# Retention of two heads at once: where the rests of queries, keys and values are taken, and the cast of the rotated keys ahead of the values in even heads

## The chip, the cores and the metric

The kernel runs on one core of one Trainium2 chip. The metric is the device time of one execution in microseconds. All times here are in microseconds (us) unless marked otherwise.

## The reference, cut to what matters

The program is a stack of one mixed block (a recurrent part, dilated attention, cross attention, a feed-forward part) and of two layers of a second block. The change touches only the retention of the second block's two layers:

```python
def retention_branch(q, k, v, g):
    qh = rotary(q.reshape(B, S, RET_HEADS, RET_DK)) * (RET_DK ** -0.5)
    kh = rotary(k.reshape(B, S, RET_HEADS, RET_DK))
    ...
    fwd = chunk_retention(qh, kh, vh, decay_logs(DECAY_OFFSET_FWD), strict=False)
    bwd = flip(chunk_retention(flip(qh), flip(kh), flip(vh), decay_logs(DECAY_OFFSET_BWD), strict=True))
    y = fwd + bwd
    y = (y - mean(y)) * rsqrt(var(y) + EPS)      # per token and head
    return y * silu(g)
```

There are four heads of width 256, 512 tokens, and a model width of 1024. Over the whole sequence, both directions together are a 512 x 512 matrix of scores (keys times queries), each multiplied by a decay that depends only on the distance of the two tokens, and then multiplied with the values. This is how the kernel computes it.

## The kernel before, in words

**Three products for one.** Every matrix product is made in full precision out of three fast ones. Each operand x is split into a high part (x cast to the rounded type) and a rest (x minus the high part); the products are high by high, high by rest and rest by high. ScalarE (ACT) makes the high parts by casts, VectorE (DVE) makes the rests of activations by subtractions, and GpSimd (POOL) makes the rests of the weights (`w_lo`, line 720, four pieces of 256 columns for a unit).

**Weights.** All weights come in units of 128 x 1024 numbers, in the order in which TensorE (PE) uses them. A unit is loaded by SyncE (SP) into one of three slots of `w_raw`, cast by ACT into one of five slots of `w_hi` (`cast_to`, line 1650) and gets its rest from POOL (`w_lo`). PE waits for the rest of a unit before the first matmul that uses it (`low_made`). Which unit ACT casts when is written into ACT's program: `follow(t)` for a tile t casts up to three units past the last unit of t, and `take_values` casts the last unit of the value tiles itself before it takes the first of them. A tile of queries, keys or gates has one unit (eight blocks of 128 x 128, 24 matmuls); the four tiles of values (one for each 128 tokens, 512 columns, that is the values of two heads at once) share four units, two blocks of each unit in each tile, so the fourth unit is first used by the seventh of the eight blocks of the first value tile.

**Order of the work.** Every engine follows its own written-out list with semaphore waits; nothing is scheduled at run time, and a waiting instruction holds all that stand behind it on its engine. PE's list for the retention of a layer is: query, key and value tiles of head 0; then for each head `hd`: its two gate tiles, a wait for the rests (`ret_low`, line 1559), the scores (lines 1566 to 1568, 24 matmuls), the two query tiles of the next head, the products with the values (lines 1580 to 1582), the first key tile of the next head, the sums of squares (line 1591), the second key tile, the spread of the inverse deviation (line 902), and, if the next head is even, its four value tiles. Values are computed in even heads for two heads: `RV` for this head and `RV_NEXT` for the one that follows.

**Between PE's tiles.** DVE rotates the queries and the keys out of PSUM (`rotate`, lines 3110 to 3115, six operations); ACT casts them to their high parts (`rotated_high`, line 2192), takes the values (`take_values`, lines 2177 and 2179 for each tile, then the cast of line 2182) or, ahead of odd heads, only casts the second half that is already there (`take_next_values`, line 2187); DVE subtracts (`rest`, line 3120) in the order query, values, key. DVE also multiplies the scores with the decay (line 3138), scales the outputs of the head with the gates (line 3154) and with the inverse deviation (line 3158), and makes their rests (line 2318). PE may start the scores of head n when 5n + 3 rests are counted: those of query, values and keys.

Of the kernel before, what the change touches and what calls it, by code (L numbers as in the profile page):

```python
# [32 lines left out]
XH = 4  # L33
# [202 lines left out]
def build_program(nc, plan, ap, out):  # L236
# [19 lines left out]
    with ctx:  # L256
# [5 lines left out]
        def sem(name):  # L262
            if name not in sems:
                sems[name] = ctx.enter_context(nc.semaphore(name))
            return sems[name]
# [151 lines left out]
        RQ = take(2, S)  # L417
        RKY = take(2, S)
        RV = take(TC, 256)
# [327 lines left out]
        def _(pe):  # L747
# [727 lines left out]
            for l in range(LAYERS):  # L1475
# [80 lines left out]
                for hd in range(XH):  # L1556
                    n = XH * l + hd
                    head_tiles(hd, "g")
                    pe.wait_ge(sem("ret_low"), 5 * n + 3)
                    for c in range(TC):  # L1560

                        if TC * n + c >= 2:
                            pe.wait_ge(sem("ret_masked"), TC * n + c - 1)
                        for k in range(2):
                            o, cols = banks[4 + c % 2][:], slice(c * P, (c + 1) * P)
                            nc.tensor.matmul(o, RK_HI[:, k, cols], RQ_HI[:, k, :], start=(k == 0), stop=False)  # L1566
                            nc.tensor.matmul(o, RK_HI[:, k, cols], RQ_LO[:, k, :], start=False, stop=False)  # L1567
                            mm = nc.tensor.matmul(o, RK_LO[:, k, cols], RQ_HI[:, k, :], start=False, stop=(k == 1))  # L1568
                        mm.then_inc(sem("ret_raw"), 1)
                    if hd + 1 < XH:  # L1570
                        head_tiles(hd + 1, "q")
                    else:
                        gate_tile(f"ret_out{l}", f"n1_{l}", 0)
                    pe.wait_ge(sem("ret_low"), 5 * n + 5)
                    if hd:
                        pe.wait_ge(sem("tmp_ready"), splits[f"ret{l}"][0] + 2 * hd)
                    for d in range(2):
                        for c in range(TC):
                            o, cols, high = banks[6 + d][:], slice(P * d, P * (d + 1)), RP_HI[:, c // 2, c % 2, :]
                            nc.tensor.matmul(o, RV_HI[:, c, cols], high, start=(c == 0), stop=False)  # L1580
                            nc.tensor.matmul(o, RV_HI[:, c, cols], RP_LO[:, c, :], start=False, stop=False)  # L1581
                            mm = nc.tensor.matmul(o, RV_LO[:, c, cols], high, start=False, stop=(c == TC - 1))
                        mm.then_inc(sem("ret_y"), 1)

                    if hd + 1 < XH:
                        tile(stages[f"ret_k{l}_{hd + 1}"][0], splits[f"n1_{l}"][0])
                    else:
                        gate_tile(f"ret_out{l}", f"n1_{l}", 1, range(0, KT // 2))
                    pe.wait_ge(sem("ret_sq_sum"), n + 1)
                    for c in range(TC):  # L1590
                        mm = nc.tensor.matmul(banks[5][:, c:c + 1], ROT[:, 2, c * P:(c + 1) * P], ones[:, 0:1], start=True,
                                              stop=True)
                    mm.then_inc(sem("ret_var"), 1)

                    if hd + 1 < XH:
                        tile(stages[f"ret_k{l}_{hd + 1}"][0] + 1, splits[f"n1_{l}"][0])
                    else:
                        gate_tile(f"ret_out{l}", f"n1_{l}", 1, range(KT // 2, KT))
                    pe.wait_ge(sem("ret_copied"), 2 * n + 2)
                    spread(banks[6])  # L1600
                    if hd + 1 < XH and hd % 2:
                        head_tiles(hd + 1, "v")
# [21 lines left out]
        def _(act):  # L1624
# [496 lines left out]
            for l in range(LAYERS):  # L2121
# [67 lines left out]
                def rotated_high(hd, i, dst, src):  # L2189

                    act.wait_ge(sem("rotated"), 2 * (XH * l + hd) + i + 1)
                    done(nc.scalar.copy(dst, src), "ret_high")

                for hd in range(XH):
                    n = XH * l + hd
                    for what in "qk":
                        for t in range(*stages[f"ret_{what}{l}_{hd}"]):
                            follow(t)
                    if hd == 0:
                        act.wait_ge(sem("gate_used"), counts["gate_ready"])  # L2200
                        act.dma_start(COS, ap["rotary"][:, 0, :]).then_inc(sem("ret_tables"), 16)
                        act.dma_start(SIN, ap["rotary"][:, 1, :]).then_inc(sem("ret_tables"), 16)
                    else:
                        act.wait_ge(sem("ret_masked"), TC * n)
                    act.dma_start(STRIP, ap["strips"][hd]).then_inc(sem("strip_landed"), 16)
                    if hd == 0:
                        rotated_high(0, 0, RQ_HI, RQ)
                        take_values(0)
                        rotated_high(0, 1, RK_HI, RKY)
                    for t in range(*stages[f"ret_g{l}_{hd}"]):  # L2210
                        i = t - stages[f"ret_g{l}_{hd}"][0]
                        if n:
                            act.wait_ge(sem("tmp_ready"), splits[f"ret{l}"][0] + 2 * hd)
                        take_tile(t, RG[:, i, :], func=ACT.Silu)
                    ahead_tiles = list(range(*stages[f"ret_q{l}_{hd + 1}"]) if hd + 1 < XH else
                                       plan.gates[f"ret_out{l}"][0][0:2])
                    follow(ahead_tiles[0])
                    for i in range(2):
                        act.wait_ge(sem("ret_masked"), TC * n + 2 * i + 2)
                        done(nc.scalar.copy(RP_HI[:, i], RP[:, 2 * i:2 * i + 2, :]), "ret_high")  # L2220
                    follow(ahead_tiles[1])
                    for d in range(2):
                        act.wait_ge(sem("ret_y"), 2 * n + d + 1)
                        done(nc.scalar.activation(ROT[:, 2 + d, :], banks[6 + d][:], ACT.Square), "ret_sq")
                    for d in range(2):
                        done(nc.scalar.copy(RY[:, d, :], banks[6 + d][:]), "ret_copied")
                    if hd + 1 < XH:
                        for t in range(*stages[f"ret_k{l}_{hd + 1}"]):
                            follow(t)
                        rotated_high(hd + 1, 0, RQ_HI, RQ)  # L2230
                        if hd % 2:
                            take_values(hd + 1)
                        else:
                            take_next_values(hd + 1)
                        rotated_high(hd + 1, 1, RK_HI, RKY)
                    for d in range(2):
                        high(splits[f"ret{l}"][0] + 2 * hd + d)
                gates(plan.gates[f"ret_out{l}"][0])
# [44 lines left out]
        def _(dve):  # L2283
# [67 lines left out]
            def spread_out():  # L2351

                dve.wait_ge(sem("spread"), counts["stats_ready"])
# [697 lines left out]
            for l in range(LAYERS):  # L3051
# [65 lines left out]
                def rest(count, dst, x, hi):  # L3117

                    dve.wait_ge(sem("ret_high"), count)
                    do(V_.tensor_tensor(dst, x, hi.bitcast(F32), ALU.subtract), "ret_low")  # L3120

                def rests(hd):

                    n = 5 * (XH * l + hd)
                    rest(n + 1, RQ_LO, RQ, RQ_HI)
                    rest(n + 2, RV_LO, RV_NEXT if hd % 2 else RV, RV_HI)
                    rest(n + 3, RK_LO, RKY, RK_HI)

                dve.wait_ge(sem("ret_tables"), 32 * (l + 1))
                rotate(0, "q", RQ)  # L3130
                rotate(0, "k", RKY)
                rests(0)
                for hd in range(XH):
                    n = XH * l + hd
                    dve.wait_ge(sem("strip_landed"), 16 * (n + 1))
# [10 lines left out]
                    dve.wait_ge(sem("ret_var"), n + 1)  # L3146
                    statistic(banks[5][:, 0:TC], 256, TC, EPS)
                    if hd + 1 < XH:
                        rotate(hd + 1, "k", RKY)
                    for t in range(*stages[f"ret_g{l}_{hd}"]):  # L3150
                        evacuated(dve, t)
                    dve.wait_ge(sem("ret_copied"), 2 * n + 2)
                    for d in range(2):
                        do(V_.tensor_tensor(RY[:, d, :], RY[:, d, :], RG[:, d, :], ALU.mult))
                    spread_out()
                    for d in range(2):
                        q = splits[f"ret{l}"][0] + 2 * hd + d
                        do(V_.tensor_tensor(tmp[:, q % 2, :], RY[:, d, :], banks[6][:], ALU.mult), "tmp_ready")
                    for d in range(2):
                        low(splits[f"ret{l}"][0] + 2 * hd + d)  # L3160
                    if hd + 1 < XH:
                        rests(hd + 1)
                for j0, j1 in ((0, KT - 2), (KT - 2, KT - 1), (KT - 1, KT)):
                    gated_pairs(f"ret_out{l}", False, j0, j1)
                    for j in range(j0, j1):
# [174 lines left out]
```

## Time and profile before

| | |
|---|---|
| median of three runs | 3012.26 us (3008.8 to 3012.26) |
| the profiled execution | 3010.7 us, its span 3008.9 us |
| PE busy | 2978.3 us, 99% of the span |
| DVE, ACT, POOL busy | 51%, 37%, 53% |
| granted TensorE clock, mean | 0.999 |
| PE waiting for the rests of line 3120 ahead of the scores | 9.9 us in 6 waits |

An engine's busy time is the time in which at least one of its instructions runs. PE counts matmuls, and PEld the loads of their stationary operands, which run beside the matmuls. Matmul ends are modelled: a matmul shows 0.39 us where the next begins 0.23 us after it.

### The profile page before, as it was taken

How to read it: one execution, taken by the hardware profiler on the slowest of the kernel's cores; microseconds unless marked ns; L12 is line 12 of the kernel's file. 1: busy time of each engine (PE TensorE's matmuls, PEld its weight loads, DVE VectorE, ACT ScalarE, POOL GpSimd, SP SyncE). 2: the span in 40 equal slices, each digit the busy share in tenths (PEclk: the TensorE clock that was granted, in tenths of full speed). 3: DMA queues.
4: the chain of work that ended last, by engine and by line, in shares of the span. 5: the costliest groups of instructions: out<-in, count | busy, mean ns of one | idle time of the engine just before them, and what ended most of it. 6: DMA issues, size and time to landing. Idle time of an engine off the chain costs nothing.

```text
span 3008.9 us, 49790 instructions
## 1 busy us (share of the span) xinstructions
PE 2978.3 (99%) x19898; PEld 2488.9 (83%) x19898; DVE 1537.9 (51%) x2179; ACT 1102.7 (37%) x1665; POOL 1589.7 (53%) x1911
## 2 busy tenths in 40 slices
PE   9999999999999999999999999999999999999998
PEld 7877777788898888988787898888988887888887
DVE  5477887435457777731334274435612443383635
ACT  4454444334442233432433243323433333342323
POOL 6423223357458777554444566556455445565654
PEclk9999999999999999999999999999999999999999
DMA  5211111333327777223222323232223222233322
GB/s 174 84 44 42 48 48 59 98 134 126 98 93 265 261 249 258 84 85 111 83 80 73 92 89 107 91 99 94 81 93 106 78 78 84 92 98 98 98 94 75
DMA packets 91749, 319.49 MB, mean 106 GB/s; under 512 B 10096, under 2 KB 14320, under 8 KB 91264
## 3 DMA queue, kind: packets, MB, share of 16 engines
q1 hardware_dynamic: 84256, 301.34, 30.7%
q10 hardware_dynamic: 7264, 14.98, 1.5%
q8 instruction: 158, 2.59, 0.4%
q14 instruction: 71, 0.58, 0.1%
HBM read 312.32 MB, written 3.93 MB: 105 GB/s over the span
## 4 chain that ended last, share of the span: by engine, by line
PE 90%; DVE 4%; POOL 3%; issue 2%; ACT 1%; DMA 0%; ACTq 0%; POOLq 0%; DVEq 0%; SPq 0%
PE bank L789 24%; PE bank L793 24%; PE bank L790 24%; POOL w_lo L720 2%; PE bank L1056 2%; PE bank L782 2%; PE bank L784 2%; PE bank L783 2%; PE bank L1067 1%; PE bank L1075 1%; DVE arena_r L3120 1%; PE bank L1566 1%; PE bank L1567 1%; PE bank L1568 1%; PE bank L1581 0%
## 5 line engine op out<-in xcount | busy, mean ns | idle before, releaser
L720 POOL TENSOR_TENSOR w_lo<-w_raw,w_hi 128x256 fp32r<-128x256 f32 x1864 | 1541.2, 861 | 1097.8 <-ACT w_hi L1650 1085.3
L789 PE MATMUL bank<-act,w_hi 128*128 128x512 f32 (+1 forms) x3776 | 1423.6, 377 | 7.2 <-POOL w_lo L720 3.9
L793 PE MATMUL bank<-act,w_lo 128*128 128x512 f32 (+1 forms) x3776 | 1401.6, 371 | 0.0
L790 PE MATMUL bank<-act,w_hi 128*128 128x512 f32 (+1 forms) x3776 | 1400.5, 371 | 0.0
L789 PEld LDWEIGHTS bank<-act,w_hi 128*128 128x128 f32 x3776 | 711.4, 188 | 140.0 <-issue 11.6
L793 PEld LDWEIGHTS bank<-act,w_lo 128*128 128x128 f32 x3776 | 711.2, 188 | 122.6
L790 PEld LDWEIGHTS bank<-act,w_hi 128*128 128x128 f32 x3776 | 712.0, 189 | 114.2
L1650 ACT CAST w_hi<-w_raw 128x1024 fp32r<-128x1024 f32 x468 | 487.3, 1047 | 458.2 <-DMA w_raw<-in_weights 202.3
L1658 ACT ACTIVATE arena<-bank 128x512 f32<-128x512 f32 (+1 forms) x177 | 104.3, 593 | 413.7 <-PE bank L793 397.1
L738 POOL TENSOR_TENSOR stats<-stats,exponent 128x8 f32<-128x8 f32 (+2 forms) x39 | 47.0, 1205 | 316.1 <-DVE stats L2349 151.3
L2318 DVE TENSOR_TENSOR act<-tmp,act 128x512 fp32r<-128x512 f32 (+1 forms) x164 | 137.1, 836 | 92.8 <-ACT act L1677 87.2
L3017 DVE SCALAR_TENSOR_TENSOR arena<-arena,small 128x1024 f32<-128x1024 f32 x93 | 140.3, 1509 | 3.3
L3179 DVE TENSOR_SCALAR arena<-arena,params 128x512 f32<-128x512 f32 x88 | 53.0, 602 | 170.2 <-ACT arena L1658 169.8
L1677 ACT CAST act<-tmp 128x512 fp32r<-128x512 f32 (+1 forms) x164 | 95.5, 585 | 121.3 <-DVE tmp L2924 32.0
L2912 DVE TENSOR_TENSOR arena<-arena,bank 128x512 f32<-128x512 f32 x32 | 22.0, 688 | 230.5 <-PE bank L793 230.5
L2485 DVE SCALAR_TENSOR_TENSOR arena<-bank,small,arena 128x512 f32<-128x512 f32 x48 | 36.1, 751 | 166.8 <-PE bank L793 166.6
L1913 ACT ACTIVATE arena<-bank 128x512 f32<-128x512 f32 (+1 forms) x104 | 64.8, 631 | 114.5 <-PE bank L1075 97.1
L3182 DVE SCALAR_TENSOR_TENSOR arena<-arena,params 128x512 f32<-128x512 f32 x88 | 83.0, 943 | 3.1
L782 PE MATMUL bank<-w_hi,act 128*128 128x512 f32 (+1 forms) x224 | 84.6, 378 | 0.0
L784 PE MATMUL bank<-w_hi,act 128*128 128x512 f32 (+1 forms) x224 | 83.7, 374 | 0.0
L783 PE MATMUL bank<-w_lo,act 128*128 128x512 f32 (+1 forms) x224 | 83.7, 374 | 0.0
L3181 DVE SCALAR_TENSOR_TENSOR arena<-arena,params 128x512 f32<-128x512 f32 x88 | 70.6, 802 | 3.1
(299 smaller groups left out, 2557.3 us busy)
## 6 DMA issues: line engine op xcount, KB each, us to landing
w_raw<-in_weights SPq DMA_DIRECT2D x469, 512.0 KB, 3.7
arena<-in_ada SPq DMA_DIRECT2D x96, 512.0 KB, 4.7
arena<-in_strips ACTq DMA_DIRECT2D x8, 448.0 KB, 4.2
arena<-in_x ACTq DMA_DIRECT2D x1, 2048.0 KB, 11.0
y_scratch<-tmp ACTq DMA_DIRECT2D x7, 256.0 KB, 2.0
arena<-y_scratch ACTq DMA_DIRECT2D x1, 1792.0 KB, 8.2
arena<-in_x SPq DMA_DIRECT2D x3, 512.0 KB, 7.7
arena<-in_lora_w ACTq DMA_DIRECT2D x8, 128.0 KB, 2.2
```

The costliest lines, as they stand in the source:

```text
L720: ins = nc.gpsimd.tensor_tensor(w_lo[:, k, cols], w_raw[:, u % RAWS, cols], w_hi[:, k, cols].bitcast(F32), ALU.subtract)
L782: nc.tensor.matmul(o, xs[0], wh, start=first, stop=False)
L783: nc.tensor.matmul(o, xs[0], wl, start=False, stop=False)
L784: mm = nc.tensor.matmul(o, xs[1], wh, start=False, stop=last)
L789: nc.tensor.matmul(o, wh, xh, start=first, stop=False)
L790: nc.tensor.matmul(o, wh, xl, start=False, stop=False)
L793: mm = nc.tensor.matmul(o, wl, xh, start=False, stop=last)
L1650: nc.scalar.copy(w_hi[:, k, :], w_raw[:, u % RAWS, :]).then_inc(sem("w_high"), 1)
L1658: nc.scalar.activation(dst, banks[bank_of(t)][:, 0:n], func, scale=scale).then_inc(sem(f"bank_free{bank_of(t)}"), 1)
L1677: ins = nc.scalar.copy(o, x) if shift is None else nc.scalar.activation(o, x, ACT.Identity, bias=shift)
L2318: do(V_.tensor_tensor(o, x, h, ALU.subtract), "low_done")
L3017: do(V_.scalar_tensor_tensor(o, w, c_act[:, k:k + 1], o, ALU.mult, ALU.add), "ada_used")
```

## The change

The work stays the same: no operation is added or taken away. Three lists are changed.

- **DVE.** `rests` is split into three functions. The query's rest goes ahead of the rotation of the next head's keys. If the next head is odd, the rest of its values follows it there. The key's rest goes behind the multiplication with the gates (line 3154 before) and ahead of the wait for the inverse deviation. If the next head is even, the values' rest stays at the end. In head 0 the order becomes query, key, values.
- **ACT.** In head 0 and ahead of every even head, the cast of the rotated keys goes ahead of `take_values`. Ahead of odd heads the order stays.
- **PE.** The wait ahead of the scores asks for 5n + 2 rests in even heads (query and key), and for 5n + 3 in odd ones as before.

```diff
-                    pe.wait_ge(sem("ret_low"), 5 * n + 3)
+                    pe.wait_ge(sem("ret_low"), 5 * n + 2 + hd % 2)
...
                     if hd == 0:
                         rotated_high(0, 0, RQ_HI, RQ)
+                        rotated_high(0, 1, RK_HI, RKY)
                         take_values(0)
-                        rotated_high(0, 1, RK_HI, RKY)
...
                         rotated_high(hd + 1, 0, RQ_HI, RQ)
                         if hd % 2:
+                            rotated_high(hd + 1, 1, RK_HI, RKY)
                             take_values(hd + 1)
                         else:
                             take_next_values(hd + 1)
-                        rotated_high(hd + 1, 1, RK_HI, RKY)
+                            rotated_high(hd + 1, 1, RK_HI, RKY)
...
+                def query_rest(hd):
+                    rest(5 * (XH * l + hd) + 1, RQ_LO, RQ, RQ_HI)
+                def key_rest(hd):
+                    rest(5 * (XH * l + hd) + 2 + hd % 2, RK_LO, RKY, RK_HI)
+                def value_rest(hd):
+                    rest(5 * (XH * l + hd) + 3 - hd % 2, RV_LO, RV_NEXT if hd % 2 else RV, RV_HI)
...
                     statistic(banks[5][:, 0:TC], 256, TC, EPS)
                     if hd + 1 < XH:
+                        query_rest(hd + 1)
+                        if hd % 2 == 0:
+                            value_rest(hd + 1)
                         rotate(hd + 1, "k", RKY)
...
                         do(V_.tensor_tensor(RY[:, d, :], RY[:, d, :], RG[:, d, :], ALU.mult))
+                    if hd + 1 < XH:
+                        key_rest(hd + 1)
                     spread_out()
...
                         low(splits[f"ret{l}"][0] + 2 * hd + d)
-                    if hd + 1 < XH:
-                        rests(hd + 1)
+                    if hd + 1 < XH and hd % 2:
+                        value_rest(hd + 1)
```

On ACT, between the rotated queries' cast ahead of head 2 and its first value tile (`act_attn<-arena` is the cast of rotated queries or keys, `w_hi<-w_raw` the cast of a weight unit, line 2177 the first piece of a value tile; a line with - is of before, with + of the change):

```order
 L1650 CAST w_hi<-w_raw 128x1024 [waits tile_done,w_landed0]
 L1650 CAST w_hi<-w_raw 128x1024 [waits tile_done,w_landed1]
-L2192 CAST act_attn<-arena 128x1024 [waits rotated]
+L2192 CAST act_attn<-arena 128x1024 [waits rotated] x2
 L1650 CAST w_hi<-w_raw 128x1024 [waits tile_done,w_landed2,ret_y]
 L2177 ACTIVATE arena<-bank 128x256 [waits tile_done]
```

The keys' cast, which waits for DVE's rotation, has moved from behind the value tiles (its old row there is gone) to ahead of one weight unit's cast, the last that the value tiles need.

On ACT in head 0 of a layer the same move:

```order
 L2202 DMA arena<-in_rotary 128x512
 L2205 DMA arena<-in_strips 128x896
-L2192 CAST act_attn<-arena 128x1024 [waits rotated]
+L2192 CAST act_attn<-arena 128x1024 [waits rotated] x2
 L1650 CAST w_hi<-w_raw 128x1024 [waits tile_done,w_landed1]
 L2177 ACTIVATE arena<-bank 128x256 [waits tile_done]
```

Here too one weight unit's cast stands behind the keys' cast now.

On DVE ahead of head 1, from the last step of the keys' rotation to the first scores' masking, before:

```order
L3115 TENSOR_TENSOR arena<-arena 128x512
L3154 TENSOR_TENSOR arena<-arena 128x512 x2
L3158 TENSOR_TENSOR tmp<-arena,bank 128x512 x2
L2318 TENSOR_TENSOR act<-tmp,act 128x512 x2
L3120 TENSOR_TENSOR arena_r<-arena,act_attn 128x1024
L3120 TENSOR_TENSOR arena_r<-arena,squares_r 128x1024
L3120 TENSOR_TENSOR arena_r<-arena,act_attn 128x1024
L3138 TENSOR_TENSOR arena<-bank,arena 128x512 x4
```

The same place in the changed kernel, from the statistic on (its DVE lines have other numbers: 3121 is the rest, 3111 to 3116 the rotation, 3162 the gates, 3168 the inverse deviation; `squares_r` are the values, `act_attn` the query or the key):

```order
L2350 TENSOR_SCALAR stats<-bank 128x4
L3121 TENSOR_TENSOR arena_r<-arena,act_attn 128x1024
L3121 TENSOR_TENSOR arena_r<-arena,squares_r 128x1024
L3111 TENSOR_TENSOR arena<-bank,table 128x512
L3112 TENSOR_TENSOR arena<-bank,arena 128x512
L3113 TENSOR_TENSOR arena<-arena 128x512
L3114 TENSOR_TENSOR arena<-bank,arena 128x512
L3115 TENSOR_TENSOR arena<-bank,table 128x512
L3116 TENSOR_TENSOR arena<-arena 128x512
L3162 TENSOR_TENSOR arena<-arena 128x512 x2
L3121 TENSOR_TENSOR arena_r<-arena,act_attn 128x1024
L3168 TENSOR_TENSOR tmp<-arena,bank 128x512 x2
```

Two rests stand ahead of the rotation now, and only two multiplications between the rotation and the key's rest. PE's list is the same in both kernels.

## Rows read from the trace of the kernel before

**Rows 1.** The page: the span and PE's busy time
```profile
span 3008.9 us, 49790 instructions
...
PE 2978.3 (99%) x19898; PEld 2488.9 (83%) x19898; DVE 1537.9 (51%) x2179; ACT 1102.7 (37%) x1665; POOL 1589.7 (53%) x1911
```

**Rows 2.** Waits of PE: line, releaser, us in total, times, longest
```profile
PE bank L1566 <- DVE arena_r L3120: 9.9, 6, 2.9
```

**Rows 3.** Timeline of PE at head 1's scores: start, us, instruction
```profile
1492.40 0.39 PE L793 MATMUL bank<-act,w_lo 128*128 128x512 f32 x1
1494.89 0.50 PE L1566 MATMUL bank<-act_attn 128*128 128x512 f32 x1 [2.10 <-DVE arena_r L3120]
...
1498.87 0.40 PE L1567 MATMUL bank<-arena_r,act_attn 128*128 128x512 f32 x1
```

**Rows 4.** Windows: length, busy PE PEld DVE ACT POOL, granted clock, DMA share, GB/s
```profile
1495.00:1497.00 2.00, 2.00 (x6) 1.57 (x7) 0.00 (x0) 0.00 (x0) 2.00 (x4) 0.58 0.00 0
1497.00:1499.00 2.00, 2.00 (x7) 1.58 (x6) 0.69 (x1) 0.00 (x0) 2.00 (x4) 0.57 0.83 258
...
1612.00:1614.00 2.00, 1.60 (x7) 1.34 (x8) 0.34 (x1) 0.00 (x0) 2.00 (x3) 1.00 0.10 16
```

**Rows 5.** Timeline of PE: first matmul of the scores of heads 2 and 3
```profile
1564.02 0.50 PE L1566 MATMUL bank<-act_attn 128*128 128x512 f32 x1 [0.34 <-DVE arena_r L3120]
...
1612.40 0.50 PE L1566 MATMUL bank<-act_attn 128*128 128x512 f32 x1 [2.89 <-DVE arena_r L3120]
```

**Rows 6.** Timeline of DVE ahead of head 1's scores
```profile
1481.55 0.69 DVE L3110 TENSOR_TENSOR arena<-bank,table 128x512 f32<-128x512 f32 x1 [5.41 <-PE bank L793]
...
1485.91 1.42 DVE L3154 TENSOR_TENSOR arena<-arena 128x512 f32<-128x512 f32 x2
1487.36 1.41 DVE L3158 TENSOR_TENSOR tmp<-arena,bank 128x512 f32<-128x512 f32 x2
1488.81 1.42 DVE L2318 TENSOR_TENSOR act<-tmp,act 128x512 fp32r<-128x512 f32 x2
1490.27 1.23 DVE L3120 TENSOR_TENSOR arena_r<-arena,act_attn 128x1024 fp32r<-128x1024 f32 x1
1491.53 1.64 DVE L3120 TENSOR_TENSOR arena_r<-arena,squares_r 128x1024 fp32r<-128x1024 f32 x1
```

**Rows 7.** Timeline of ACT in the same stretch
```profile
1473.97 1.06 ACT L2187 CAST squares_r<-arena 128x1024 fp32r<-128x1024 f32 x1
1485.91 1.05 ACT L2192 CAST act_attn<-arena 128x1024 fp32r<-128x1024 f32 x1 [10.88 <-DVE arena L3115]
```

**Rows 8.** Issues of DMA in 1604 to 1614: engine, KB, us to landing
```profile
arena<-in_strips ACTq DMA_DIRECT2D x1, 448.0 KB, 4.3
```

**Rows 9.** Timeline of ACT, then DVE, then PE ahead of head 2
```profile
1522.15 1.06 ACT L2192 CAST act_attn<-arena 128x1024 fp32r<-128x1024 f32 x1
1524.33 1.05 ACT L1650 CAST w_hi<-w_raw 128x1024 fp32r<-128x1024 f32 x1 [1.12 <-PE bank L793]
...
1535.03 1.42 DVE L3154 TENSOR_TENSOR arena<-arena 128x512 f32<-128x512 f32 x2
...
1534.96 0.39 PE L782 MATMUL bank<-w_hi,act 128*128 128x512 f32 x1
```

**Rows 10.** Timeline of ACT in head 0 of the first layer
```profile
1413.34 1.05 ACT L2192 CAST act_attn<-arena 128x1024 fp32r<-128x1024 f32 x1 [8.22 <-DVE arena L3115]
1414.30 1.05 ACT L1650 CAST w_hi<-w_raw 128x1024 fp32r<-128x1024 f32 x1
```

**Rows 11.** Timeline of POOL there
```profile
1405.20 2.83 POOL L720 TENSOR_TENSOR w_lo<-w_raw,w_hi 128x256 fp32r<-128x256 f32 x4 [2.61 <-ACT w_hi L1650]
1415.42 3.28 POOL L720 TENSOR_TENSOR w_lo<-w_raw,w_hi 128x256 fp32r<-128x256 f32 x4 [7.39 <-ACT w_hi L1650]
```

**Rows 12.** Timeline of DVE, then of PE there
```profile
1414.97 0.69 DVE L3110 TENSOR_TENSOR arena<-bank,table 128x512 f32<-128x512 f32 x1 [1.66 <-PE bank L793]
...
1418.78 0.47 PE L782 MATMUL bank<-w_hi,act 128*128 128x512 f32 x1
```

More of the change, by code:

```diff
@@ L3120, in rest @@
                     do(V_.tensor_tensor(dst, x, hi.bitcast(F32), ALU.subtract), "ret_low")
[L3122 to L3127, printed above, removed]
+                def query_rest(hd):
[4 more added lines that the diff above has]
+                    rest(5 * (XH * l + hd) + 3 - hd % 2, RV_LO, RV_NEXT if hd % 2 else RV, RV_HI)
                 dve.wait_ge(sem("ret_tables"), 32 * (l + 1))
@@ L3131, in _ @@
                 rotate(0, "k", RKY)
-                rests(0)
+                query_rest(0)
+                key_rest(0)
+                value_rest(0)
                 for hd in range(XH):
```

## The prediction

> **What bounds the kernel now.** I read the page first: PE is busy for 2978.3 us of a span of 3008.9 [rows 1], so only what makes PE wait, or run slower, can change the time. A gain is at most what PE idles at the changed place, and any new wait of PE is added in full, since nothing behind it has slack to give back.
>
> Next the waits of PE. The largest group is the one the change aims at: the scores (line 1566) wait six times for DVE's rests (line 3120), 9.9 us in all, 2.9 at most [rows 2]. These are the heads with a head in front of them, three in each layer. In the first layer the idle times are 2.10, 0.34 and 2.89 for heads 1, 2 and 3 [rows 3, 5].
>
> Then what such a wait costs. Matmuls follow each other every 0.23 us, while each shows 0.39, so the busy time hides 0.16 of a gap; and the first matmul after a gap takes 0.1 longer to its successor than usual. At head 1 the last gate matmul begins at 1492.40, the next could have begun at 1492.63, and began at 1494.89 [rows 3]: 2.26, that is 2.10 and 0.16. Behind this gap the granted clock is 0.58 and 0.57 for two windows, the lower of its two levels (1.2 GHz instead of 2.4) [rows 4]: from 1494.89 to 1498.87 PE makes ten steps in 3.98 us [rows 3] where ten of 0.23 take 2.3. Less the 0.1, the low clock costs 1.6. Behind the longer gap ahead of head 3 the clock stays at 1.00 [rows 4], and the mean of the whole execution is 0.999 (the 4 us at 0.57 are all that is missing), so this was one case of six.
>
> Last, the chain that ends the wait at head 1, on DVE [rows 6]: rotation from 1481.55 to 1485.91, gates, inverse deviation, two rests of the outputs, and then three rests from 1490.27, each 1.23 to 1.64.
>
> **Part 1, the odd heads (1 and 3 of each layer): the wait goes.** DVE is idle for 5.41 us ahead of the rotation [rows 6]. The casts of the query and of the values run there already: the values' cast ends at 1473.97 + 1.06 = 1475.03, the query's stands in front of it [rows 7]. Two rests of at most 1.64 each, 3.3 us, fit into the 5.41, and the rotation starts when it did. Behind it come two gate multiplications, to 1487.36 [rows 6]; the keys' cast, begun at 1485.91 with 1.05 [rows 7], is done by 1486.96. The key's rest ends by 1487.36 + 1.64 = 1489.0. PE arrives at 1492.63, so there are 3.6 us to spare and the wait is zero.
>
> What is late next here: the inverse-deviation step, the output's casts and the strip's DMA stand 1.2 to 1.6 us later, since ACT issues the strip behind those casts. The strip takes 4.3 us to land [rows 8]. At head 1 the step of line 3158 now ends at 1487.36 + 1.64 + 1.41 = 1490.4, the strip lands at about 1494.7, and the first masking would otherwise begin near 1492.63 + 1.8 = 1494.4 (an estimate from 24 matmuls in four groups of six at 0.23, plus the result's way out). PE's third group of scores needs that masking only at 1492.63 + 0.1 + 12 x 0.23 = 1495.5. I take 0, and 0.5 for each of the four heads as the other end.
>
> **Part 2, head 2 of each layer: the small wait goes too.** The scores no longer need the values' rest, and the query's and key's are made under the value tiles (4 x 24 x 0.23 = 22 us). Its 0.34 is gone.
>
> Removed in all: 9.9 + 6 x (0.16 + 0.1) = 11.5, and 1.6 of low clock: **13.1 us**.
>
> **Part 3, ACT's list in even heads: a new wait.** The keys' cast waits for DVE's rotation, and behind it in ACT's list now stands the cast of the fourth unit of the value tiles. ACT is in order, POOL makes that unit's rest behind the cast, and PE needs it at the seventh block of the first value tile, its 19th matmul. In head 0 of the first layer before: unit cast at 1414.30 [rows 10], rest on POOL from 1415.42 to 1418.70 [rows 11], the 19th matmul at 1418.78 [rows 12]. It is just in time: there is no cover at all. With the change:
> - DVE's rotation of the keys starts at 1414.97 [rows 12] and takes 4.36 (1481.55 to 1485.91 [rows 6]): 1419.33.
> - The keys' cast starts there. The next cast starts 0.96 later (1413.34 to 1414.30 [rows 10]): 1420.29.
> - POOL starts 1.12 after the cast's start (1414.30 to 1415.42 [rows 10, 11]): 1421.41. Its four pieces take 2.83 to 3.28 [rows 11]: the longer one ran beside DVE's subtractions. Only a piece of the key's rest is beside it here, so I take 2.95: 1424.36.
> - PE goes on 0.08 later (1418.70 to 1418.78), at 1424.44. New wait: 5.66, and 5.5 to 6.0 between the bounds.
>
> Ahead of head 2: before, the fourth unit is cast at 1524.33, as soon as a unit was free, and has 10.6 us until the 19th matmul at 1534.96 [rows 9]. Now the rotation ends at 1535.03 [rows 9] (the gates' step starts there, as the keys' cast did in head 1). Unit cast 1535.99, POOL 1537.11; the key's rest lies beside it on DVE, so 3.28: 1540.39, PE 1540.47. New wait: 5.51, at 2.83 it would be 5.06.
>
> The second layer has the same lists and, in the waits, the same sizes; I take the same: 2 x (5.66 + 5.51) = 22.3, and 4 x 0.1 for the first steps: **22.7 us**. The weights behind (the gates' units) are cast relative to the end of the first value tile, and move with it. The value tiles, the gate tiles and the scores all come later by the wait; ACT, DVE and POOL gain slack and PE doesn't.
>
> **Clock.** The new gaps are 5.1 us or more, twice the one that was followed by a slow stretch; one of six gaps between 0.3 and 2.9 was followed by one. No row shows a gap of this size in a dense stretch of PE. Bounds: 0 (as behind 2.89) and 3.2 each (two slow stretches). I take one slow stretch of 1.6 for each of the four, **6.4 us**, as the gap is well above the one that had it. The Trainium skill (TensorE: Matmul & The Clock Gate, HAM oscillation — how this bites in real kernels) says that waiting inside a stream of matmuls sends the clock back to its half rate, at every repetition. By that rule all four gaps pay; the trace agrees in one of the six shorter gaps, and has none as long. If it did not hold here, the sum would be 6.4 lower.
>
> For POOL's two durations the Trainium skill (GPSIMD Engine Reference, Specifications) has GpSimd's SBUF interface shared with VectorE, with contention when a VectorE instruction has two SBUF inputs. The rests have two. By it the 3.28 applies ahead of head 2, as taken; without it both layers together would be 0.9 lower.
>
> **Sum.** 3010.7 (the profiled execution's own time, 0.05% below the median of 3012.26) - 13.1 + 22.7 + 6.4 = **3026.7 us**, 0.5% slower. About 0.2%, 6 us, is what a measurement of this kernel can tell from no change.
>
> **Rivals.**
> - **The new waits stay, the clock doesn't fall.** For it: the 2.89 gap with a clock of 1.00 [rows 4]. Against: the 2.10 gap with 0.57. Time: 3020.3. Chance 0.23.
> - **Faster: the fourth unit is not late.** Were its cast still done ahead of the keys' (some other tile's `follow` reaching it), only parts 1 and 2 would be left: 3010.7 - 13.1 = 2997.6. For it: ahead of head 2 the unit had 10.6 us of cover [rows 9]. Against: ACT's list has the cast behind the keys' in all four places, and the rotation ends after PE's need in both. It decides the sign from the point where the four waits together fall under 13 us, 3.3 each: the rotation would have to end 2 to 3 us earlier, but it can't start before the second key tile is done. Chance 0.05.
> - **The odd heads keep a wait.** The strip lands late and holds masking and thus the third group of scores: 0.5 each, or the early rests delay the rotation. Time: 3026.7 + 2 = 3028.7, at worst 3033 with low clock behind such gaps. Chance 0.12.
> - **New and old waits cancel,** so that the time stays within 0.2% (up to 3016.7). For that the four new waits would have to add 19 us or less, 4.7 each with any low clock in it; the shortest by the bounds is 5.06 without it. Chance 0.05.
>
> **How the numbers follow.** The forecast has the remaining 0.55. Its own range is 3023 to 3031: POOL's bounds give -1 to +1, the clock's placement -3 to +3. Down to the case without low clock and a base of 3008.8 (the lowest of the runs): 3020.3 - 1.9 - 0.9 = 3017.5. Up: 3026.7 + 2 for the strips, + 3.2 for a second slow stretch at two gaps, + 0.8 for POOL's upper bound: 3032.7. Faster 0.05, same 0.05, slower 0.90.
>
> **What would show it.** In the profile after: no wait of line 1566 for the rest; instead four waits of the value tiles' line 782 for POOL's `w_lo`, or for the cast in front of it, 5.1 to 6.0 each, in heads 0 and 2 of each layer; the keys' cast right ahead of the weight cast on ACT, its wait on the rotation's last step; a granted clock below 1 in the windows behind these gaps. DVE: two rests in the idle time ahead of the rotation of odd heads, and the rotation's start unchanged. A 19th matmul of the value tile without a gap, or a wait at 1566 that remains, would prove me wrong.

## The result and the profile after

| | before | changed |
|---|---|---|
| median | 3012.14 us (4 runs, 3008.8 to 3012.26) | 3027.69 us (4 runs, 3026.98 to 3028.2) |
| span of the profiled execution | 3008.9 us | 3025.7 us |
| mean granted TensorE clock | 0.999 | 0.994 |

The ratio is 1.0054, with a 95% interval of 1.0037 to 1.0072: slower by 15.6 us, and clear of noise. The forecast was 3026.7 us.

The page of the changed kernel, its span and its busy times, which answer to [rows 1]:

```profile
span 3025.7 us, 49790 instructions
...
PE 2986.3 (99%) x19898; PEld 2496.4 (83%) x19898; DVE 1536.5 (51%) x2179; ACT 1101.9 (36%) x1665; POOL 1590.9 (53%) x1911
```

Same instructions, and PE is busy 8 us longer: that is the slower clock, since no matmul was added. The waits of PE in the changed kernel (line, releaser, us, times, longest), for [rows 2]:

```profile
PE bank L782 <- POOL w_lo L720: 21.6, 4, 5.5
PE bank L789 <- DVE act L2321: 1.9, 8, 0.2
PE bank L789 <- POOL w_lo L720: 1.6, 2, 1.0
```

The group of line 1566 that led this list is gone altogether. In its place stand four waits of the value tiles for the rest of their weights, at twice its total (21.6 us against 9.9). The head 0 of the first layer shows how each comes about. First ACT, then POOL, then PE, to set against [rows 10 to 12]:

```profile
1417.60 1.05 ACT L2192 CAST act_attn<-arena 128x1024 fp32r<-128x1024 f32 x1 [4.65 <-DVE arena L3116]
1418.55 1.04 ACT L1650 CAST w_hi<-w_raw 128x1024 fp32r<-128x1024 f32 x1
...
1419.67 3.04 POOL L720 TENSOR_TENSOR w_lo<-w_raw,w_hi 128x256 fp32r<-128x256 f32 x4 [13.36 <-ACT w_hi L1650]
...
1422.75 0.79 PE L782 MATMUL bank<-w_hi,act 128*128 128x512 f32 x1 [5.54 <-POOL w_lo L720]
```

The cast of the weight unit (1418.55) stands right behind the keys' cast, which waited 4.65 us for DVE's rotation. Before, it stood behind the query's cast and had nothing to wait for. Ahead of head 2, for [rows 9]:

```profile
1537.40 1.05 ACT L2192 CAST act_attn<-arena 128x1024 fp32r<-128x1024 f32 x1 [11.82 <-DVE arena L3116]
1538.36 1.04 ACT L1650 CAST w_hi<-w_raw 128x1024 fp32r<-128x1024 f32 x1
...
1539.47 3.23 POOL L720 TENSOR_TENSOR w_lo<-w_raw,w_hi 128x256 fp32r<-128x256 f32 x4 [8.17 <-ACT w_hi L1650]
...
1542.76 0.79 PE L782 MATMUL bank<-w_hi,act 128*128 128x512 f32 x1 [5.27 <-POOL w_lo L720]
```

What follows the gap is a slow stretch. Windows of PE in the changed kernel (length, busy, granted clock, DMA share, GB/s), behind the gap in head 0 and then behind the one ahead of head 2:

```profile
1423.00:1425.00 2.00, 2.00 (x5) 0.50 0.64 164
1425.00:1427.00 2.00, 2.00 (x6) 0.50 0.24 98
1427.00:1429.00 2.00, 2.00 (x8) 0.85 0.00 0
...
1543.00:1545.00 2.00, 2.00 (x5) 0.50 0.60 176
1545.00:1547.00 2.00, 2.00 (x6) 0.50 0.21 86
1547.00:1549.00 2.00, 2.00 (x10) 0.98 0.00 0
```

All four gaps have one. Its end in head 0, in PE's timeline, is where the steps go back from 0.43 to 0.23:

```profile
1427.19 0.59 PE L783 MATMUL bank<-w_lo,act 128*128 128x512 f32 x1
1427.61 0.40 PE L784 MATMUL bank<-w_hi,act 128*128 128x512 f32 x1
1427.84 0.40 PE L782 MATMUL bank<-w_hi,act 128*128 128x512 f32 x1
```

From 1422.75 to 1427.61 PE makes 11 steps, which take 4.86 us and would take 2.5 at full clock: 2.4 lost. The other three gaps read in the same way lose 2.1, 2.5 and 2.2 (10, 12 and 10 steps in 4.38, 5.22 and 4.44 us): 9.1 in all, the longer first step of each included.

The odd heads went as the prediction had it. DVE of the changed kernel ahead of head 1, for [rows 6]:

```profile
1482.47 1.39 DVE L3121 TENSOR_TENSOR arena_r<-arena,act_attn 128x1024 fp32r<-128x1024 f32 x1
1483.90 1.65 DVE L3121 TENSOR_TENSOR arena_r<-arena,squares_r 128x1024 fp32r<-128x1024 f32 x1
1487.85 0.69 DVE L3111 TENSOR_TENSOR arena<-bank,table 128x512 f32<-128x512 f32 x1 [2.31 <-PE bank L793]
...
1493.66 1.22 DVE L3121 TENSOR_TENSOR arena_r<-arena,act_attn 128x1024 fp32r<-128x1024 f32 x1
```

The two early rests fit into the idle time and leave 2.31 of it; the key's rest ends at 1494.88, 4 us ahead of PE, whose first score begins at 1498.93 without a gap.

**The account of the two profiled executions.** New waits: 21.6, and 4 x 0.16 that the busy time hides: 22.2. Slow stretches: 9.1. Less 13.1 for the old waits and their slow stretch: +18.2. The spans differ by 16.8. The rest of the difference was there ahead of the changed place: the keys' rotation of head 0 starts at 1413.25 here and at 1414.97 before [rows 12], 1.7 us sooner, in a part of the program that is the same in both. 18.2 - 1.7 = 16.5. Those 1.7 us are chiefly waits of line 789 for POOL, all of which lie ahead of the changed place: 1.6 us above, and in the kernel before

```profile
PE bank L789 <- POOL w_lo L720: 3.9, 5, 1.4
```

Against them stands one more slow stretch, at 1229.6 in the changed kernel and in a part that the change does not touch; it cost 1.1 us there.

### The profile page after: what moved, and what is told of

Its sections match the earlier page's. It is cut to its first block, busy times and chain, and to the rows that moved or that the text cites. A ratio compares the mean times of both kernels' runs of the same rounds, so it can differ in the third digit from the quotient of the medians.

```text
span 3025.7 us, 49790 instructions
## 1 busy us (share of the span) xinstructions
PE 2986.3 (99%) x19898; PEld 2496.4 (83%) x19898; DVE 1536.5 (51%) x2179; ACT 1101.9 (36%) x1665; POOL 1590.9 (53%) x1911
## 4 chain that ended last, share of the span: by engine, by line
PE 92%; issue 3%; DVE 2%; POOL 2%; ACT 0%; DMA 0%; POOLq 0%; DVEq 0%; ACTq 0%; SPq 0%
PE bank L789 25%; PE bank L793 25%; PE bank L790 25%; PE bank L1056 2%; PE bank L782 2%; POOL w_lo L720 1%; PE bank L1067 1%; PE bank L783 1%; PE bank L784 1%; PE bank L1075 1%; PE bank L1568 0%; PE bank L1566 0%; PE bank L1567 0%; DVE act L2321 0%; PE bank L1486 0%
## 5 line engine op out<-in xcount | busy, mean ns | idle before, releaser
L782 PE MATMUL bank<-w_hi,act 128*128 128x512 f32 (+1 forms) x224 | 89.0, 397 | 21.6 <-POOL w_lo L720 21.6
L784 PE MATMUL bank<-w_hi,act 128*128 128x512 f32 (+1 forms) x224 | 86.8, 388 | 0.0
```

What stands on the lines that cost most here:

```text
L782: nc.tensor.matmul(o, xs[0], wh, start=first, stop=False)
L784: mm = nc.tensor.matmul(o, xs[1], wh, start=False, stop=last)
```

## The experiments

The theory (A in the expectations): the whole loss is one cast in the wrong place on ScalarE, and everything else in the change is a gain. The main rival (B): the loss comes from the rests' new places on VectorE, or from the keys' cast itself. Two more rivals are named in the expectations: C is about which of VectorE's moves are needed and whether the early rests do harm, D says that head 0 has some slack that the rows hide. The first four kernels share 15 runs of the kernel before on their chip (median 3013.55), the last four 18 (3012.48).

### The weight unit's cast first

The changed kernel with one line more in each of the two places:

```diff
                         rotated_high(0, 0, RQ_HI, RQ)
+                        cast_to(tiles[stages[f"ret_v{l}_{hd}"][0]]["blocks"][-1][0])
                         rotated_high(0, 1, RK_HI, RKY)
                         take_values(0)
...
                         if hd % 2:
+                            cast_to(tiles[stages[f"ret_v{l}_{hd + 1}"][0]]["blocks"][-1][0])
                             rotated_high(hd + 1, 1, RK_HI, RKY)
                             take_values(hd + 1)
```

> The changed kernel with one difference: in head 0 and ahead of even heads ScalarE casts the fourth unit of the value tiles first, then the rotated keys. Theory A (all of the loss is that unit's late cast, 22 us of waits and some 9 us of low clock behind them, against a gain of 13 us): about 13 us under the kernel before (2999), no waits of line 782 for the rest of the weights, no waits of line 1566. Rival B (the loss comes from the rests on VectorE in their new places, or from the keys' cast itself): stays within 5 us of the changed kernel (3023 to 3028).

Measured: 2997.48 us (5 runs, 2997.09 to 2999.92), ratio to before 0.9953 (0.994 to 0.9965). That is 30 us under the changed kernel (measured on another chip; the two ratios to before differ by the same 1.0%), for the place of four casts. ACT of this kernel in head 0 and then ahead of head 2:

```profile
1414.63 1.05 ACT L2192 CAST act_attn<-arena 128x1024 fp32r<-128x1024 f32 x1 [8.25 <-DVE arena L3118]
1415.59 1.05 ACT L1650 CAST w_hi<-w_raw 128x1024 fp32r<-128x1024 f32 x1
1420.91 1.05 ACT L2192 CAST act_attn<-arena 128x1024 fp32r<-128x1024 f32 x1 [4.27 <-DVE arena L3118]
...
1521.70 1.05 ACT L1650 CAST w_hi<-w_raw 128x1024 fp32r<-128x1024 f32 x1 [1.10 <-PE bank L793]
1532.42 1.05 ACT L2192 CAST act_attn<-arena 128x1024 fp32r<-128x1024 f32 x1 [9.67 <-DVE arena L3118]
```

The waits for the rotation are still there (4.27 and 9.67 us), and the keys are still cast ahead of the values; only nothing that PE needs soon stands behind them. No wait of line 782 or 1566 is left. Theory A holds, and B falls: both the rests' new places and the keys' early cast are still in this kernel.

### VectorE's list alone

The kernel before, with DVE's rests as in the change, except that in even heads the values' and the key's rest both stay at the end; ACT's list and PE's counts are those of before:

```diff
                     if hd + 1 < XH:
+                        query_rest(hd + 1)
+                        if hd % 2 == 0:
+                            value_rest(hd + 1)
                         rotate(hd + 1, "k", RKY)
...
+                    if hd + 1 < XH and hd % 2 == 0:
+                        key_rest(hd + 1)
                     spread_out()
...
-                    if hd + 1 < XH:
-                        rests(hd + 1)
+                    if hd + 1 < XH and hd % 2:
+                        value_rest(hd + 1)
+                        key_rest(hd + 1)
```

> The kernel before with the change of VectorE's list alone: the query's rest ahead of the keys' rotation, in odd heads the values' too, the key's rest of odd heads behind the gates; in even heads values' and key's rest stay at the end; ScalarE's list and TensorE's counts as before. Theory A: 13 us under the kernel before (2999), all six waits of line 1566 gone. Rival B: slower than before, by up to 16 us. Rival C (the odd heads' early rests delay the rotation, or the strip lands late): 3 to 8 us under it.

Measured: 2997.14 us (5 runs, 2995.97 to 2998.73), ratio 0.995 (0.9938 to 0.9963), 16.4 us faster. The waits of PE in this kernel begin with what was second before:

```profile
PE bank L789 <- POOL w_lo L720: 3.2, 4, 1.7
PE bank L789 <- DVE act L2320: 1.9, 8, 0.2
```

So the even heads need nothing from ACT's new order: one rest less at the end is enough for their small wait too. Like the kernel of the experiment above, this one beats both the kernel before and the changed one.

### ScalarE's order alone

The kernel before with the keys' cast ahead of the values in even heads. All rests stay at the end, but in even heads in the order query, key, values, and PE's count for even heads is the changed kernel's. The lines of VectorE's order are not shown:

```diff
-                    pe.wait_ge(sem("ret_low"), 5 * n + 3)
+                    pe.wait_ge(sem("ret_low"), 5 * n + 2 + hd % 2)
...
+                        rotated_high(0, 1, RK_HI, RKY)
                         take_values(0)
-                        rotated_high(0, 1, RK_HI, RKY)
...
                         if hd % 2:
+                            rotated_high(hd + 1, 1, RK_HI, RKY)
                             take_values(hd + 1)
```

> The kernel before with ScalarE's keys ahead of the values in even heads alone (rests all at the end as before, in even heads in the order query, key, values, and TensorE's count for them). Theory A: four new waits of line 782, 5.3 to 5.7 each, and low clock of about 2.3 behind each, less the small wait of heads 2: 31 - 1 = 30 us over the kernel before (3042), waits of line 1566 in odd heads still there. Rival B: within 3 us of the kernel before (3012).

Measured: 3042.27 us (4 runs, 3041.67 to 3043.67), ratio 1.01 (1.0086 to 1.0113), 28.7 us over before. PE's waits:

```profile
PE bank L782 <- POOL w_lo L720: 20.7, 4, 5.5
PE bank L1566 <- DVE arena_r L3121: 9.2, 4, 2.9
```

The parts add up within the noise: -16.4 and +28.7 make +12.3, and the whole change measured +15.6 (interval 11 to 22). The small waits of heads 2 are removed by either part and so count twice in the sum; that is 1.2 us of the difference. The windows of PE in this kernel hold something that I had not expected:

```profile
1500.00:1515.00 15.00, 13.68 (x53) 0.89 0.33 105
1545.00:1560.00 15.00, 13.62 (x53) 0.89 0.21 72
1620.00:1635.00 15.00, 12.11 (x47) 0.89 0.36 123
2385.00:2400.00 15.00, 12.91 (x51) 0.89 0.21 65
2430.00:2445.00 15.00, 10.19 (x40) 0.89 0.14 51
2505.00:2520.00 15.00, 12.90 (x58) 0.99 0.11 32
```

The stretches at 1500, 1620, 2385 and 2505 are the scores of the odd heads, with the old waits of 2.1 to 2.9 us. In this execution each of them has a granted clock below 1 in its window; in the profiled execution of before only one had.

### Only head 2 mended

The changed kernel with the second of the two `cast_to` lines of the first experiment alone:

```diff
                         if hd % 2:
+                            cast_to(tiles[stages[f"ret_v{l}_{hd + 1}"][0]]["blocks"][-1][0])
                             rotated_high(hd + 1, 1, RK_HI, RKY)
```

> The changed kernel with the fourth unit's cast first ahead of head 2 only; head 0 of each layer stays as changed. Theory A: two waits of 5.5 us and their low clock are left, two are gone: 15 to 16 us under the changed kernel, so within 2 us of the kernel before (3012). Rival B: as the changed kernel (3028). If the low clock behind a wait were no part of it, only 11 us would go (3017).

Measured: 3013.18 us (10 runs, 3010.7 to 3016.17), ratio 1.0 (0.9991 to 1.001). PE's waits have two of the four left:

```profile
PE bank L782 <- POOL w_lo L720: 11.1, 2, 5.5
PE bank L789 <- POOL w_lo L720: 4.7, 4, 2.5
```

From 2997.5 to 3013.2 (both on one chip) are 15.7 us for two gaps, 7.9 each. Of these 5.7 are idle (11.1 / 2, and the 0.16 that the busy time hides); the remaining 2.1 or so are what the slow stretch behind each costs. That is near the price found in the timeline of the changed kernel (2.1 to 2.5), here from medians.

### Two rests early, the key's at the end

As VectorE's list alone, but the key's rest stays last in every head (the edit is shown against that kernel):

```diff
-                    if hd + 1 < XH and hd % 2 == 0:
-                        key_rest(hd + 1)
                     spread_out()
...
-                    if hd + 1 < XH and hd % 2:
-                        value_rest(hd + 1)
+                    if hd + 1 < XH:
+                        if hd % 2:
+                            value_rest(hd + 1)
                         key_rest(hd + 1)
```

> VectorE's list changed less than in the run of its list alone: query's and (odd heads) values' rest ahead of the keys' rotation, but the key's rest stays at the very end in every head. Theory A (PE arrives at 2.3 to 3.0 us ahead of the last rest, and the two rests moved away take 2.5 to 3.3): 12 to 13 us under the kernel before (2999 to 3000), at most 0.3 us of wait left in head 3. Rival C (the key's rest has to move too): 3 to 8 us under it.

Measured: 2999.02 us (4 runs, 2996.63 to 3001.38), ratio 0.9955 (0.994 to 0.9969). No wait of line 1566 is left. Moving the key's rest adds nothing that these runs can tell: with it the ratio to before was 0.995 (0.9938 to 0.9963), on another chip, and the intervals overlap.

### Only the key's rest moved

The complement: query's and values' rests at the end, the key's behind the gates in odd heads.

```diff
+                    if hd + 1 < XH and hd % 2 == 0:
+                        key_rest(hd + 1)
                     spread_out()
...
                     if hd + 1 < XH:
-                        rests(hd + 1)
+                        query_rest(hd + 1)
+                        value_rest(hd + 1)
+                        if hd % 2:
+                            key_rest(hd + 1)
```

> Only the key's rest of odd heads moves behind the gates; query's and values' rests stay at the end. Theory A (VectorE has the same work between rotation and scores, only in another order): within 2 us of the kernel before (3012), waits of line 1566 about 10 us as before. Rival C: 3 to 13 us under it.

Measured: 3006.26 us (9 runs, 3003.89 to 3010.12), ratio 0.998 (0.9971 to 0.999), 6.2 us faster. The expectation by theory A (within 2 us of before) missed. PE's waits, and then DVE's three rests ahead of head 1, the key's first:

```profile
PE bank L1566 <- DVE arena_r L3120: 6.7, 4, 1.7
```

```profile
1485.77 1.23 DVE L3120 TENSOR_TENSOR arena_r<-arena,act_attn 128x1024 fp32r<-128x1024 f32 x1
...
1489.93 1.23 DVE L3120 TENSOR_TENSOR arena_r<-arena,act_attn 128x1024 fp32r<-128x1024 f32 x1
1491.19 1.63 DVE L3120 TENSOR_TENSOR arena_r<-arena,squares_r 128x1024 fp32r<-128x1024 f32 x1
```

The key's rest in the kernel before, last of the three:

```profile
1493.20 1.64 DVE L3120 TENSOR_TENSOR arena_r<-arena,act_attn 128x1024 fp32r<-128x1024 f32 x1
```

"The same work in another order" is not the same time. At the end of the chain the key's rest runs beside POOL's subtractions and takes 1.64; in the new place POOL is idle and the same rest takes 1.23. That makes each odd head's wait 0.4 shorter, 1.6 us in all. The waits fall by 3.2, from 9.9 to 6.7 us, and each is now at most 1.7. The other half is not the move itself: query's rests that stayed in their place also ran shorter in this execution, ahead of head 3 of the first layer 1.23 instead of 1.67 (an idle time of 0.39 in DVE's chain is gone there as well), and ahead of head 2 of each layer it took 1.22 and 1.23 instead of 1.81, which is why the small waits there are gone too. In the shorter cases the query's rest began no later than POOL's first piece.

The remaining 3 us of the 6.2 are the clock. Its mean over the nine runs is 0.9983, and 0.9971 over the 18 of before. A thousandth less is a stretch of 6 us at half the clock, 3 us lost where PE is busy, so an estimate from these means is 3.8 us, good to about 1. Behind the four waits of this execution no slow stretch follows.

### One and three idle copies ahead of the cast

If head 0 has no slack at all, as the prediction read it, every delay of the unit's cast must come back as a wait of PE. This is the first experiment's kernel, with copies of 128 x 1024 on ACT ahead of the unit's cast in head 0:

```diff
                         rotated_high(0, 0, RQ_HI, RQ)
+                        for _ in range(1):
+                            done(nc.scalar.copy(RG, table[:, 0:1024].rearrange("p (a s) -> p a s", s=S)), "pad", wait=True)
                         cast_to(tiles[stages[f"ret_v{l}_{hd}"][0]]["blocks"][-1][0])
```

> The changed kernel with the fourth unit cast first, and ahead of that cast in head 0 of each layer one idle copy of 128 x 1024 on ScalarE (about 1.2 us with its wait). Theory A (the unit has no cover in head 0): two waits of about 1.2 us, 2.4 to 3 us over the run without the copy, no low clock behind them. Rival D (head 0 has a cover that the rows hide): under 1 us over it.

> The same with three idle copies (3.5 us). Theory A: two waits of about 3.5 us: 7 to 8 us over the run without copies if the clock stays up, 10 to 12 if each wait is followed by a slow stretch of 1.6 to 2.4. Rival D: under 5 us.

Measured: 3000.28 us with one copy (4 runs, 2999.17 to 3001.01) and 3012.21 with three (10 runs, 3009.93 to 3014.78), against 2997.48 without: +2.8 and +14.7. The kernel without copies ran on the other chip, though; set against the runs of before on each one's own chip, the three are 16.1, 12.2 and 0.3 us under it, which makes +3.9 and +15.8. PE's waits with one copy:

```profile
PE bank L782 <- POOL w_lo L720: 2.7, 2, 1.4
```

and with three, with POOL and DVE in head 0:

```profile
PE bank L782 <- POOL w_lo L720: 9.5, 2, 5.0
```

```profile
1419.12 3.30 DVE L3125 TENSOR_TENSOR arena_r<-arena,act_attn 128x1024 fp32r<-128x1024 f32 x2
...
1418.58 5.10 POOL L720 TENSOR_TENSOR w_lo<-w_raw,w_hi 128x256 fp32r<-128x256 f32 x4 [10.76 <-ACT w_hi L1650]
```

One copy of 1.1 us gives two waits of 1.3 and 1.4: head 0 has no cover, and D falls. Three copies end above the expected 10 to 12, for a reason that the rows show. The later start puts most of POOL's four pieces beside DVE's two rests. The pieces take 5.10 instead of 2.83, and the rests 3.30 instead of the 2.48 that they took in the changed kernel. The wait is 5.0 where the copies are 3.2 long. In the two layers the waits are 9.5 + 0.3 us; that leaves 4.9 to 6.0 for two slow stretches by the medians, and in the profiled execution's timeline the two cost 2.6 and 1.7.

## Why the prediction was right, and which term was off

- **The bound and the removed wait: right.** PE's idle time at line 1566 went to zero, and by DVE's two early rests, as costed; the strip's DMA, late by a good microsecond, held nobody.
- **The new wait: right in its place and its size.** Forecast 22.3 us in four waits of 5.5 and 5.7; measured 22.2. POOL's four pieces were taken as 2.95 in head 0 and 3.28 ahead of head 2, and were 3.04 and 3.23. The reading behind the larger one was loose: the 3.28 of [rows 11] ran beside the keys' rotation, of which only line 3112, a subtraction, was longer (0.98 instead of 0.69), and not beside a rest. It came close all the same. The fourth unit's cast was found by reading ACT's list from the keys' cast downward, and asking who needs the next item.
- **The slow clock behind the gaps: mechanism right, size too small.** The term "one slow stretch of 1.6 for each of the four" with the first steps came to 6.8 and measured 9.1 (2.3 for each gap). The step that failed is taking the price from the one stretch seen before: there ten steps were slow, behind the new gaps 10 to 12, with a first step of 0.6 instead of 0.34 (the first step of a wait with no slow clock behind it). The prediction also took that one stretch for all that is missing from the mean of 0.999; the last 4.9 us of the execution were at the lower level too, with PE idle, so this cost nothing.
- **The gain: too small as well, for the same reason.** 13.1 was worked out from one profiled execution with one slow stretch. Over the runs VectorE's part alone measured 16.4 (11 to 19). The 33 runs of the kernel before show why: with a mean granted clock of 0.999 they took 3006.7 and 3009.8 us, with 0.996 3012.3 to 3018.1. The execution whose rows the prediction rests on had 0.999, which only two of the 33 had. The means agree: 0.9971 over the 15 runs of before on that chip and 0.9988 over the five of VectorE's part are an estimated 5.0 us of slow clock, and with the 11.5 of the waits that makes 16.5.
- **Luck.** The gain was 3.3 too small, the slow stretches 2.3 too small, and the base 3010.7 was 1.5 below the median. These errors nearly cancel, so 3026.7 against 3027.69 flatters the working.
- **The rivals.** The clock did not stay up: all four gaps had a slow stretch. "The fourth unit is not late" was wrong for the change, but is exactly what the first experiment builds, and its 2997.6 was measured as 2997.48. That match is luck too: the kernel was 16.1 us under the runs of before on its chip (3013.55), not 13.1 under 3010.7. The odd heads kept no wait.
- **The two places drawn from the Trainium skill.** For the clock (the Trainium skill, TensorE: Matmul & The Clock Gate, HAM oscillation — how this bites in real kernels) the trace agrees in four of four gaps; also the shorter old waits were followed by a low clock in one of six in one execution, and in four of four odd-head waits in another. For the interface that GpSimd shares with VectorE (the Trainium skill, GPSIMD Engine Reference, Specifications) the trace agrees, with POOL's four pieces at 2.83 alone, 3.04 and 3.23 partly beside rests, and 5.10 mostly beside them.

What stays open: when exactly a wait is followed by a slow stretch. In the retention parts of all the profiled executions one follows each of the 12 waits of 4.5 to 5.5 us, five of the eight of 2.1 to 2.9 us (one of four in the kernel before, four of four with ScalarE's order alone), and none of the six of 1.3 to 1.7 us. Why the same wait of 2.1 us has one in one execution and not in another, no kernel here took apart.

Slow stretches also come without such a wait. The one near 1230 us, behind an idle time of only 0.3 us in the changed kernel, is there in all six profiled executions of kernels with ScalarE's list edited and in none of the four others, although the edits lie behind it. It cost about 1.1 us in the changed kernel, and no run tells whether that pattern is chance.

## What to carry to other kernels

When an instruction that waits is moved ahead in a hand-written list, read the engine's list behind it item by item until the old place, and ask for each item when its consumer needs it: here four casts of 1 us each that belonged to another stream cost 30 us by standing behind a rotation. And try the parts of such a change alone: VectorE's half was worth 16 us, and ScalarE's half was needed for none of it.

## What the runs showed of the hardware

- An idle gap of TensorE can cost more than itself: behind the four gaps of 5.3 to 5.5 us in the changed kernel the clock was 0.50 until 10 to 12 matmuls later, 2.1 to 2.5 us each, so the price of such a wait was about 1.4 times its length.
- Two-input subtractions on VectorE and GpSimd slow each other by more than the first rows told. In the rows of these runs, GpSimd's four pieces took 2.83 to 5.20 us, VectorE's rest 1.22 to 1.81. Where a rest stands in the list changes how long it takes.
- Runs of one kernel can differ by how much of them the slow clock takes: 33 runs of the kernel before spread over 11.4 us, the slowest with the lowest mean clock. Two kernels without the old waits spread over 2.8 us in five runs each, but the one with two rests early over 4.8 in four, so that the waits are the whole cause of the spread is not shown.
